# GpSimd takes over the scaling of probabilities in three attention stages of a fused two-block kernel

## The reference, cut to what matters

```
logits = q @ k.T * scale + bias            # 128 queries x keys, causal, window or memory
p      = softmax(logits)                    # exp(logits - max) * (1 / sum)
out    = gate * (p @ v)                     # gate: sparse branches of block one only
```

## Time and profile before

| what | value |
|---|---|
| runs | 1303.8, 1309.54 and 1895.66 us, median 1309.54 |
| profiled execution: span, first to last instruction | 1299.3 us |
| lowest run less that span | 4.5 us |
| mean granted TensorE clock of the profiled execution | 0.921 |
| PE, DVE, ACT, POOL busy | 88, 52, 43, 30% |
| first attention ("ab") | 176 to 340 us |
| differential and memory maps ("dm") | 1040 to 1130 us, the four memory maps from 1092 us |
| latent attention ("mla") | 1195 to 1256 us |

### The profile page before, as it was taken

The page is one execution under the profiler, slowest core; times in us unless marked ns, Lnnn a source line. Parts: engine busy times, 40 slices in busy tenths (PEclk is TensorE's granted clock), DMA queues, the critical chain, the costliest instruction groups (busy, mean ns, idle before and its releaser), DMA issues.

```text
span 1299.3 us, 16304 instructions
## 1 busy us (share of the span) xinstructions
PE 1141.9 (88%) x5378; PEld 953.7 (73%) x5378; DVE 681.0 (52%) x1485; ACT 555.6 (43%) x1138; POOL 390.9 (30%) x172
## 2 busy tenths in 40 slices
PE   5939678999999999999999999998996886755989
PEld 3828567888888878788888888886885675645767
DVE  6204648787433356444444442223757367667851
ACT  5212468676322234344444433234333455434631
POOL 2314530000144444344444444445343400010013
PEclk9969688998999999999999999999998956866899
DMA  4353330000022222222222233233221200000003
GB/s 167 90 141 106 105 110 21 26 17 17 33 97 97 93 88 98 77 97 97 97 97 97 97 130 114 81 114 101 93 82 65 82 16 1 1 33 16 1 17 113
DMA packets 38610, 98.23 MB, mean 76 GB/s; under 512 B 11884, under 2 KB 14060, under 8 KB 38380
## 3 DMA queue, kind: packets, MB, share of 16 engines
q1 hardware_dynamic: 33680, 88.06, 20.7%
q10 hardware_dynamic: 4876, 9.49, 2.1%
HBM read 95.30 MB, written 5.88 MB: 78 GB/s over the span
## 4 chain that ended last, share of the span: by engine, by line
issue 63%; POOL 14%; PE 13%; DVE 7%; ACT 2%; POOLq 1%; ACTq 0%; DVEq 0%
POOL WLO L457 14%; PE PS L1363 4%; PE PS L1364 3%; PE PS L1365 3%; DVE BLO L900 1%; PE PS L1501 1%; DVE PB L1004 1%; PE PS L1630 1%; DVE PB L1039 1%; DVE PB L1101 1%; ACT PB L624 1%; POOLq L453 0%; DVE BLO L1276 0%; DVE HLO L1276 0%; ACT BHI L765 0%
## 5 line engine op out<-in xcount | busy, mean ns | idle before, releaser
L457 POOL TENSOR_TENSOR WLO<-RAW,WHI 128x1024 fp32r<-128x1024 f32 x160 | 388.5, 2429 | 897.0 <-ACT WHI L471 896.9
L471 ACT ACTIVATE WHI<-RAW 128x1024 fp32r<-128x1024 f32 x160 | 169.4, 1059 | 381.4 <-PE PS L1365 335.6
L1363 PE MATMUL PS<-HHI,WHI 128*128 128x512 f32 x648 | 256.9, 396 | 39.8 <-POOL WLO L457 25.2
L1364 PE MATMUL PS<-HLO,WHI 128*128 128x512 f32 x648 | 254.6, 393 | 0.0
L1365 PE MATMUL PS<-HHI,WLO 128*128 128x512 f32 x648 | 254.4, 393 | 0.0
L1363 PEld LDWEIGHTS PS<-HHI,WHI 128*128 128x128 f32 x648 | 123.0, 190 | 70.2 <-POOL WLO L457 25.3
L1363 PE MATMUL PS<-BHI,WHI 128*128 128x512 f32 x368 | 144.3, 392 | 1.6 <-DVE BLO L900 1.2
L1365 PE MATMUL PS<-BHI,WLO 128*128 128x512 f32 x368 | 143.9, 391 | 0.0
L1364 PE MATMUL PS<-BLO,WHI 128*128 128x512 f32 x368 | 143.8, 391 | 0.0
L1365 PEld LDWEIGHTS PS<-HHI,WLO 128*128 128x128 f32 x648 | 123.1, 190 | 26.2
L1364 PEld LDWEIGHTS PS<-HLO,WHI 128*128 128x128 f32 x648 | 123.1, 190 | 25.6 <-issue 0.5
(11 more groups left out here) (226 smaller groups left out, 1677.1 us busy)
## 6 DMA issues: line engine op xcount, KB each, us to landing
RAW<-wstream SPq DMA_DIRECT2D x160, 512.0 KB, 3.2
X<-xT ACTq DMA_DIRECT2D x4, 512.0 KB, 7.8
bias_b<-bias_rows SPq DMA_DIRECT2D x1, 2048.0 KB
FX<-bias_b ACTq DMA_DIRECT2D x8, 256.0 KB, 2.5
outT<-X ACTq DMA_DIRECT2D x8, 256.0 KB, 2.9
bias_a<-bias_rows SPq DMA_DIRECT2D x1, 1024.0 KB
FX<-bias_a ACTq DMA_DIRECT2D x8, 128.0 KB, 2.1
FX<-memT ACTq DMA_DIRECT2D x1, 1024.0 KB, 4.8
```

Of the source, the lines that this page charges most:

```text
L457: pool.tensor_tensor(WLO[:, s, :], RAW[:, s, :], WHI[:, s, :].bitcast(F), ALU.subtract).then_inc(split_lo, 1)
L471: act.activation(WHI[:, c % 2, :], RAW[:, c % 2, :], ACT.Copy).then_inc(split_hi, 1)
L1363: pe.matmul(dst, a[0], b[0], start=first, stop=False, **kw)
L1364: pe.matmul(dst, a[0], b[1], start=False, stop=False, **kw)
```

## The change

In all maps but the differential ones the multiplies of L1039 move from DVE to POOL, with the same slices, in the same order and groups. DVE's last small operation on the weights (the reciprocal, or its product with the gate) raises a new semaphore `weighed`; POOL waits for it, multiplies, and raises `normed`, for which PE waits as before. For compressed maps DVE goes on alone after that: gate, mask and the 128x128 multiply (L1031), which raises a second new semaphore `cmp_normed`; PE waits for it ahead of the transpose of that tile. The gate operation of L1018 is now followed by a wait of its own. POOL's loop over the units is cut in four, with the three attention groups between the parts: the attention of "ab" stands behind the split of the first two units of "merge", that of "dm" behind the two of "uq", that of "mla" behind the first two of "wout2".

```diff
@@ POOL @@
+            def normalise(name):
+                maps = GROUP[name][0]
+                A = ATT[name]
+                for m in maps:
+                    if "weighed" not in m:
+                        continue
+                    pool.wait_ge(A["weighed"], m["weighed"])
+                    for qs in m["groups"]:
+                        for q in [q for q in qs if q < 4]:
+                            ap = prob_of(m, q)
+                            ins = pool.tensor_scalar(ap, ap, stat(m, WT)[:, q:q + 1], None, ALU.mult)
+                        ins.then_inc(A["normed"], 1)
+            lows(0, UNIT["merge"] + 2)
+            normalise("ab")
+            lows(UNIT["merge"] + 2, UNIT["ukv"])
+            normalise("dm")
+            lows(UNIT["ukv"], UNIT["wout2"] + 2)
+            normalise("mla")
+            lows(UNIT["wout2"] + 2, NU)
@@ DVE, normed @@
-                link(dve.reciprocal(stat(m, WT), stat(m, SUM)))
+                ins = dve.reciprocal(stat(m, WT), stat(m, SUM))
...
+                    link(ins)
+                    ins = dve.tensor_tensor(w4, w4, GATE[:, :, m["gate"]], ALU.mult)
+                if "weighed" in m:
+                    ins.then_inc(A["weighed"], 1)
+                    if "cmp" in m:
+                        c4 = stat(m, WT)[:, 4:8]
+                        link(dve.tensor_tensor(c4, c4, GATE[:, :, m["cmp"]], ALU.mult))
+                        link(dve.tensor_tensor(c4, c4, MSK[:, :], ALU.mult))
+                        p4 = prob_cmp(m).rearrange("p (q c) -> p q c", q=NT)
+                        dve.tensor_tensor(p4, p4, c4[:, :, None].broadcast_to([P, NT, 32]), ALU.mult).then_inc(A["cmp_normed"], 1)
+                    return
@@ PE, turn @@
+                                pe.wait_ge(A["cmp_normed"], m["y"] - 7)
                                 ins = pe.transpose(PS[:, 5, 256:384], prob_cmp(m), IDN[:, :])
```

More of the change, by code:

```diff
@@ L187, in build @@
         ATT = {g: {s: sem(f"{g}_{s}") for s in
-                   ("scores", "biased", "exped", "normed", "turned", "p_hi", "p_lo", "pv", "y_f", "y_hi", "y_lo")}
+                   ("scores", "biased", "exped", "weighed", "cmp_normed", "normed", "turned", "p_hi", "p_lo", "pv", "y_f", "y_hi", "y_lo")}
                for g in ("ab", "dm", "mla")}
@@ L290, in build @@
                     m["yf"] = m["y"] - 3 if maps is dm else m["y"] + 1
+                if not m.get("diff"):
+                    m["weighed"] = i + 1 if maps is not dm else m["y"] - 3
                 at, m["p"] = 0, []
@@ L452, in _, with low, lows @@
             pool.wait_ge(consts, 4)
[L453 to L457, removed]
+            def low(n, i, s):
+                pool.wait_ge(split_hi, n + 1)
+                pool.tensor_tensor(WLO[:, s, :], RAW[:, s, :], WHI[:, s, :].bitcast(F), ALU.subtract).then_inc(split_lo, 1)
+            def lows(c0, c1):
+                for c in range(c0, min(c1, c0 + c0 % 2)):
+                    low(c, 0, c % 2)
+                a, b = (c0 + 1) // 2, c1 // 2
+                if b > a:
+                    with pool.Fori(a, b) as i:
+                        for s in range(2):
+                            low(2 * i + s, i, s)
+                if c1 % 2:
+                    low(c1 - 1, 0, 0)
+            def normalise(name):
[17 more added lines that the diff above has]
+            lows(UNIT["wout2"] + 2, NU)
         @block.scalar
@@ L1013, in normed @@
                     link(dve.tensor_tensor(stat(m, SUM), stat(m, SUM), stat(m, SINK), ALU.add))
-                link(dve.reciprocal(stat(m, WT), stat(m, SUM)))
+                ins = dve.reciprocal(stat(m, WT), stat(m, SUM))
                 w4 = stat(m, WT)[:, 0:4]
[L1016 to L1019, removed]
                 if "gate" in m:
-                    link(dve.tensor_tensor(w4, w4, GATE[:, :, m["gate"]], ALU.mult))
-                if "cmp" in m:
-                    link(dve.tensor_tensor(c4, c4, MSK[:, :], ALU.mult))
+                    link(ins)
[9 more added lines that the diff above has]
+                    return
+                link(ins)
                 if m.get("mode") == "sub":
```

5 lines of the change are left out of this document (removed).

## The result

The changed kernel took 1338.3 us (median of 4 runs, 1335.66 to 1342.27) against 1304.38 us for the kernel before on the same chip (median of 3 runs; a fourth, of 1895.66 us, lies far outside them and is left out here and in the ratio, though the median of 1309.54 us given ahead of the change counts it): ratio 1.026, 95% interval 1.0227 to 1.0294. It is slower by more than two per cent, and the forecast had 1290 us. The profiled execution took 1342.27 us, with a span of 1340.4 us against 1299.3, and a mean granted clock of 0.899 against 0.921.

What follows compares the result with a forecast made beforehand. No engine full in windowed maps, PE nearly full in causal ones, DVE the bound in latent attention. Gains 6.8 + 3.0 + 0.7 + 6.5 = 17.0 us off the 1299.3 span gave 1282.3, predicted 1290 us; range 1273 to 1304.

Steps and rivals of the forecast that it cites:

- POOL's price: POOL's four multiplies of a causal map: 1.8 us by the select's row, 3.0 us as the other end.
- Rival 1: Shared path between POOL and DVE: DVE work with two SBUF inputs waits for POOL; 1302 us, chance 0.08.
- Rival 2: POOL's multiply is dear and sets the steps: 1380 us at 6.1 us a map, slower than before; chance 0.06.
- DVE's relief: A causal map's four multiplies leave DVE's queue ahead of p_lo: 1.2 us a map.
- the handovers: From DVE to POOL and from POOL to PE: 0.08 us each.
- the gains in the steps: Odd causal maps of the first attention gain 6.8 us in sum, latent attention 6.5 us.
- What was added to the span: Whole kernel: the lowest run stands 4.5 us above the profiled span and the median 10.2, added to 1282.3.
- Windowed maps, 3.0 us: First attention's windowed part: PE's waits for p_lo go, ACT is the next limit; 3.0 us, between 0 and 4.6.
- Memory maps, 0.7: Multiplies mostly not on the path, only the last map gains: 0.7 us, between 0 and 1.1.
- Rival 3: PE's clock rises with the gaps gone, 6 to 8 us on top: 1280 us, chance 0.17.
- What the profile was to show: 144 multiplies on POOL, 512 columns near 0.6 us, causal pairs 12.9 us, latent steps 5.1, PE's waits below 5.
- The two signs named for being wrong: In the new profile: POOL above 2.8 us a map, or PE's transposes waiting for POOL.

Runs made afterwards that it cites:

- probe kernel: The kernel before, with fifteen extra POOL instructions ahead of the first weight unit, none changing a result: 1318.27 us in its one run.
- short multiply: The changed kernel, but POOL multiplies only the first quarter of each tile's columns, all handovers kept: 1291.82 us, ratio 0.9909 to the kernel before.
- cheap form: The changed kernel, but POOL multiplies by the column broadcast as a second tensor: 1296.54 us, ratio 0.9928 to the kernel before.
- dear form: POOL's multiply with the weight column as scalar, as in the changed kernel: 1338.3 us, ratio 1.026 to the kernel before.

## Why the prediction was wrong, point by point

**POOL's price: this step failed.** The forecast took 1.8 us a causal map from the select's row, "because the new instruction also reads one tensor and writes one". It measured 4.26 us, above the 3.0 us given as the other end, too. Reading and writing one tensor each doesn't make two forms alike: a copy over 512 columns takes 0.61 us, the multiply 1.57 with a column and 1.49 with a constant. The subtraction of the earlier trace rows, 2.37 ns a column, was the nearer row by chance; it too stands for no general two-tensor price, since the one with a broadcast column takes 1.04 us for 512. Both rows were of another operation, and the forecast's totals at the two prices, 1290 us and the 1302 of Rival 1, both lay inside the range, so a price above both had no place in it. The Trainium skill, page "GPSIMD Engine Reference", section "4.1 Engine selection", calls a one-input operation on this engine roughly line-rate, which is to say about as fast as data can stream through. The copy, 0.61 us for 512 columns, may fit that; the multiply by a constant, also of one input, at 1.49 us doesn't.

**Rival 2 was the case, and its sum left the clock out.** It said that POOL above 2.8 us a map sets odd causal steps and above 3.3 us latent ones, and that 3.6 ns a column would cost 29 us. With 4.26 us a causal map, 3.3 ns a column all in, the same limits give 11.7 us for the odd maps, 2.1 for the even and 7.7 for the latent ones, 21.5 us and the windowed maps' share; the medians differ by 34 us. The odd step grew by 1.39 us where the limit gives 1.46, the latent one by 0.8 where it gives 0.96: the mechanism is right, step by step. What its sum lacks is the time at the lower clock. That its 29 us lie near the measured loss is in part luck. It was given 0.06 because it was priced by "twice the subtraction's rate"; the same mechanism with 4.3 us deserved a far larger share once the row's end stood at 3.04 and its limit at 2.8. Its terms were rough: the even maps, put at 2.1 us each for 6.1 us of POOL, lose nothing at the full clock (8.06 us before, 8.05 in the change with four products in each wait). The windowed part, put at 1 us a map, lost 9.5 us in eight; but the probe kernel, with nothing on POOL, lost 6.7 there at the same time on the lower clock (33.7 and 33.8 us). By that comparison of single traces some 2.8 us are POOL's, and why the clock fell in the windowed part stays open.

**DVE's relief, the handovers and the gains in the steps: right.** The 1.2 us left DVE; POOL starts 0.09 us after the reciprocal's end (1264.79 and 1264.88), and PE 0.06 us after POOL's (284.58 and 284.64), against 0.08 us forecast. With a quick POOL the causal and latent parts gave 7.7 and 7.6 us against 6.8 and 6.5. The whole gave 12 us and not 17, in the main because the windowed term wasn't there.

**What was added to the span.** The forecast set the total 4.5 to 10.2 us above the profiled span. Each later run shows 1.8 to 1.9 us between its own time and its own span, so these figures were mostly the spread between executions. It is a matter of a few us.

**Windowed maps, 3.0 us: not there.** 45.3 us with the short multiply, 44.3 in the cheap form, 44.0 before. The forecast named ACT as the next limit and still took most of the wait. With times at the lower clock of 17.9, 13.6 and 13.7 us, the last two compare best. **Memory maps, 0.7: 0**, 26.2 us in both.

**Rival 3, the clock: it mattered, with the other sign.** It counted on gaps going away. In the causal part the new waits of 0.9 to 1.0 us, two in each odd map, came with 34.4 us at the lower level in place of 10.2, and filling them took 9 us off that part in the traces. Some 20 us more in the windowed part came in the probe kernel too, without any of the waits. In the cheap form, with waits of 0.6 us at most on PE, the causal part ran at a mean clock of 1.00. Where the clock falls still varies from kernel to kernel (0.95 with the short multiply), and I can't say what share of it an execution of the change would lose by itself. The Trainium skill, page "TensorE: Matmul & The Clock Gate", section "Part 1: The HAM clock gate", ties the clock to how busy PE has been; the causal stretch agrees, 0.94 with the waits filled and 0.85 with them open, and the windowed one shows that more than these waits decides.

**Rival 1, a shared path: there, with another size and place.** L1059 and L1061 (the L1023 and L1031 of before) are stretched by 0.1 us a map together in the change and by 0.6 us in the cheap form, and it is hidden in even maps. It decides only where DVE keeps multiplies of PB beside POOL (282 to 510 ns, 351 to 647). The Trainium skill, page "SBUF — State Buffer", section "Who interferes with whom", counts both kinds, two SBUF inputs and a multiply by a column in its two-port mode, as contending with this engine under an exclusive lock, by which the second waits until the first instruction ends. Beside the cheap form the runs agree, with mask products of 602 ns that end with POOL's instruction. Beside the dear form they don't: both kinds end inside a POOL instruction that runs on, the compressed tile's after 392 ns in place of 286 and the 128-column multiply after 720 in place of 282.

**What the profile was to show.** 144 multiplies on POOL: yes, 64 + 24 + 24 + 32. One of 512 columns near 0.6 us: 1.563. Causal pairs at 12.9: 15.2, had both steps been at the full clock (7.13 and 8.06). Latent steps at 5.1: 6.93. The two signs named for being wrong, POOL above 2.8 us a map and L1537 waiting for POOL, are both there; PE's waits for it came to 32.2 us where all of them were to be below 5. Still open are the 4.9 us between the first attention and the differential maps; 6.8 us more at the lower level make about 3.4 of them.

## What to carry to other kernels

Price work that moves to another engine by its own form there, in an idle corner of the same kernel, before counting what it frees: here the forms for one product lie at 1.57 and 1.04 us, and the nearest-looking row at 0.61. Beside the price, write down the burst at which the new engine becomes the step's end (2.8 us here, by the forecast); if the bounds of the price reach across it, the losing case isn't a remote one. When two engines share a row of multiplies, let the second start after the first is done or give it all of them; side by side both slowed down (282 to 510 ns on DVE, 1563 to 1672 on POOL).

## What the runs showed of the hardware

- POOL's multiply by a column of weights, float32: 2.5 ns a column and some 0.28 us, the same in an idle corner of the kernel (1.57 us for 512 columns) and in attention (1.563). By a constant: 1.49 us for 512. The same product with the column broadcast as a second tensor: 401 to 1038 ns for 128 to 512 columns, 1.66 ns a column. A copy of 512 columns: 0.61 us.
- The two forms disturb DVE differently: the 128x4 mask product took 176 ns beside the dear form and 602 ns beside the cheap one, where it ended with POOL's instruction (163 ns alone).
- DVE's multiply of 128 columns of SBUF took 510 ns in place of 282 with POOL's single multiply beside it, and POOL's took 1672 ns in place of 1563.
- Two waits of PE of about 1 us in every second step of the causal part came with a mean granted clock of 0.85 there, where it was 0.95 before; four small products in each of the waits brought 0.94. The windowed part stood at a mean of 0.67 both in the changed kernel and in the probe kernel, which has no such waits.
